# Expert products of two mixture-of-experts layers in full fp32, on column halves of the array, with a ring of 14 expert blocks

## What is computed

```python
def moe(h, router_w, router_b, w_gate, w_up, w_down):
    x = h.reshape(-1, D)                          # 256 x 1024
    aff = jax.nn.sigmoid((x @ router_w).astype(jnp.float32))
    ...                                           # best of 4 groups of experts, then the best 2 experts in it
    w = aff * chosen
    w = (w / w.sum(-1, keepdims=True)).astype(x.dtype)
    y = jnp.zeros_like(x)
    for e in range(N_EXPERTS):                    # 16; gate and up 1024 x 512, down 512 x 1024
        he = (jax.nn.silu(x @ w_gate[e]) * (x @ w_up[e])) @ w_down[e]
        y = y + w[:, e:e + 1] * he
```

## Time and profile before

| | |
|---|---|
| runs | 1465.07, 1466.48 and 1457.2 us, median 1465.07 |
| span of the profiled execution | 1454.6 us (its own time is not given apart from the span; the median is 10.5 us above it) |
| PE, DVE, ACT busy | 1381.8, 1126.3, 932.6 us |
| mean granted TensorE clock | 0.982 |
| DMA | 342.63 MB, mean 236 GB/s |
| chain that ended last | PE 78%, DVE 11%, ACT 5%, DMA 3% |

### The profile page before, as it was taken

The page is one execution under the profiler, slowest core; times in us unless marked ns, Lnnn a source line. Parts: engine busy times, 40 slices in busy tenths (PEclk is TensorE's granted clock), DMA queues, the critical chain, the costliest instruction groups (busy, mean ns, idle before and its releaser), DMA issues.

```text
span 1454.6 us, 18747 instructions
## 1 busy us (share of the span) xinstructions
PE 1381.8 (95%) x7320; PEld 1146.0 (79%) x7320; DVE 1126.3 (77%) x1351; ACT 932.6 (64%) x1103; POOL 72.7 (5%) x78
## 2 busy tenths in 40 slices
PE   7999998999999899999899999979999998799998
PEld 5887886888888677666788888857788887699986
DVE  4765578999999777677999999976665557578872
ACT  4453545989898643584789898955545664356561
POOL 0000000000000000000000000000773000000000
PEclk9999998999999999998999999999999999899999
DMA  9644544999999934503699999956445434455550
GB/s 338 198 146 145 198 164 154 390 376 391 387 398 401 351 127 139 185 1 145 239 396 384 380 394 398 398 213 202 145 146 173 146 117 145 155 178 187 191 172 31
DMA packets 128477, 342.63 MB, mean 236 GB/s; under 512 B 10189, under 2 KB 17021, under 8 KB 111869
## 3 DMA queue, kind: packets, MB, share of 16 engines
q1 hardware_dynamic: 121632, 331.57, 62.8%
q10 hardware_dynamic: 6748, 9.77, 2.0%
HBM read 340.27 MB, written 1.05 MB: 235 GB/s over the span
## 4 chain that ended last, share of the span: by engine, by line
PE 78%; DVE 11%; ACT 5%; DMA 3%; issue 2%; ACTq 1%; DVEq 0%
PE PS L656 22%; PE PS L1287 17%; PE PS L503 9%; PE PS L581 6%; DVE wlo L468 5%; PE PS L559 5%; PE PS L1326 3%; ACT whi L462 3%; PE PS L1276 2%; DMA raw<-in_moe_w_gate 2%; PE PS L1364 2%; PE PS L1360 1%; PE PS L2023 1%; PE PS L1750 1%; PE PS L1776 1%
## 5 line engine op out<-in xcount | busy, mean ns | idle before, releaser
L468 DVE TENSOR_TENSOR wlo<-raw,whi 128x2048 fp32r<-128x2048 f32 x314 | 706.8, 2274 | 122.4 <-ACT whi L462 116.4
L462 ACT ACTIVATE whi<-raw 128x2048 fp32r<-128x2048 f32 x314 | 589.8, 1897 | 44.4 <-PE PS L559 17.3
L1287 PE MATMUL PS<-whi,xg 128*128 128x512 f32 x512 | 205.6, 402 | 0.0
L1287 PE MATMUL PS<-wlo,xg 128*128 128x512 f32 x512 | 200.5, 392 | 0.0
L656 PE MATMUL PS<-whi,th 128*128 128x512 f32 x480 | 193.5, 403 | 2.1 <-DVE wlo L468 2.0
L656 PE MATMUL PS<-whi,tl 128*128 128x512 f32 x480 | 190.2, 396 | 0.0
L656 PE MATMUL PS<-wlo,th 128*128 128x512 f32 x480 | 189.3, 394 | 0.0
L1287 PEld LDWEIGHTS PS<-whi,xg 128*128 128x128 f32 x512 | 96.4, 188 | 18.6
L1287 PEld LDWEIGHTS PS<-wlo,xg 128*128 128x128 f32 x512 | 96.3, 188 | 18.6
L656 PEld LDWEIGHTS PS<-whi,th 128*128 128x128 f32 x480 | 90.2, 188 | 25.1 <-issue 2.4
L656 PEld LDWEIGHTS PS<-whi,tl 128*128 128x128 f32 x480 | 90.1, 188 | 21.8
(11 more groups left out here) (404 smaller groups left out, 2264.9 us busy)
## 6 DMA issues: line engine op xcount, KB each, us to landing
raw<-in_moe_w_gate SPq DMA_DIRECT2D x64, 1024.0 KB, 7.5
raw<-in_moe_w_up SPq DMA_DIRECT2D x64, 1024.0 KB, 8.4
raw<-in_moe_w_down SPq DMA_DIRECT2D x64, 1024.0 KB, 7.7
raw<-in_w_in SPq DMA_DIRECT2D x32, 1024.0 KB, 5.2
raw<-in_ret_w_in SPq DMA_DIRECT2D x24, 1024.0 KB, 5.1
raw<-in_w_up SPq DMA_DIRECT2D x20, 1024.0 KB, 5.1
raw<-in_w_down SPq DMA_DIRECT2D x10, 1024.0 KB, 5.0
raw<-in_ret_w_out SPq DMA_DIRECT2D x8, 1024.0 KB, 5.0
```

Of the source, the lines that this page charges most:

```text
L462: nc.scalar.activation(s.whi[:, high, 0:kc, 0:wide], s.raw[:, slot, 0:kc, 0:wide], ACT.Copy).then_inc(s.hi_done, 1)
L468: nc.vector.tensor_tensor(s.wlo[:, slot, 0:kc, 0:wide], s.raw[:, slot, 0:kc, 0:wide], s.whi[:, high, 0:kc, 0:wide], ALU.subtract).then_inc ...
L1287: last = nc.tensor.matmul(PS[:, bank, :], stationary(c), w[:, q, c, :], start=(start and c == 0 and k == 0), stop=(stop and c == KC - 1 an ...
```

## The change

- `xg` and `hT` are kept in fp32 and not split; gate, up and down are multiplied in fp32, straight from the loaded blocks: `split_hi` and `split_lo` of expert blocks are gone (192 of the 314 pairs of splits).
- The stationary operand has 64 columns. Gate's output goes to partitions 0 to 63 of a PSUM bank and up's to 64 to 127 of the same bank (`gate_and_up`), so the two use different column halves of the array and follow each other chunk by chunk. In `down` the two halves of the output's columns stand in the same way in bank 6.
- ACT takes Silu from the one half, DVE multiplies by the other (both 64x512), 4 transposes turn the result (`turned_hidden`), ACT copies it to `hT`. The fold matmuls are gone.
- `y_split` holds, per half, the high part in 64 partitions and the low part in the other 64, so `scatter` needs 4 matmuls.
- Order on PE for an expert: gate and up, gather, scatter of the last expert, transposes of hidden, slot weights of the next expert, down.
- The blocks of an expert lie in a ring of 14: the 7 slots of `raw`, the 5 of `whi`, and two more. Counts of their own (`moe_ready`, `moe_used`) serve it; the blocks of the linear behind wait for the last use of their place (`after_experts`). Down's blocks are now 256 whole rows, two per partition, one run of 8 KB.
- The output stages ahead of a layer no longer split two expert blocks.

```diff
+MOE_SLOTS = 14
...
-        xg = A("xg", [P, 2, DC, PER, 2, SLOTS], F32R)
+        xg = A("xg", [P, 2, DC, PER, SLOTS])
...
+        moe_more = A("moe_more", [P, MOE_SLOTS - RAWS - HIGHS, KC, BW])
...
+        moe_homes = [("raw", 0), ("raw", 1), ("raw", 2), ("high", 0), ("raw", 3), ("high", 1), ("raw", 4), ("high", 2),
+                     ("raw", 5), ("high", 3), ("raw", 6), ("high", 4), ("more", 0), ("more", 1)]
...
         def out_and_norm_scalar(act, l, layer):
 
-            for i in (2, 3, 4):
+            for i in (2, 3):
                 split_hi(act, sweep_first, l.b0 + i, 0)
             early_table(ACT.Sqrt)
             root_half(act, 4 * layer, 0)
-            split_hi(act, sweep_first, l.b0 + 5, 0)
...
             residual_half(dve, o, l, 0, 0)
-            split_lo(dve, sweep_first, l.b0 + 4, 0)
             residual_half(dve, o, l, 0, 1)
...
             residual_half(dve, o, l, 1, 0)
-            split_lo(dve, sweep_first, l.b0 + 5, 0)
...
+            return [g[0:half], u[0:half], g[half:], u[half:], d[0:SEQ], d[SEQ:]]
 
         def paired_sync(sp, layer):
             b0 = moe_b0[layer]
-            for n, (e, i) in enumerate(paired_order()):
-                load_block(sp, sweep_first, b0 + n, 0, [(expert_blocks(layer, e)[i], KC, 0, BW)], block_rows(i))
+            for n in range(MOE_BLOCKS):
+                kind, k = moe_homes[n % MOE_SLOTS]
+                if n >= MOE_SLOTS:
+                    sp.wait_ge(moe_used, MOE_BLOCKS * layer + n - MOE_SLOTS + 1)
+                elif kind == "raw":
+                    sp.wait_ge(block_used, b0 + k - RAWS + 1)
+                elif kind == "high":
+                    sp.wait_ge(block_used, b0 + k - HIGHS + 1)
+                else:
+                    sp.wait_ge(block_used, b0)
...
+            def gate_and_up(e, half):
+
+                g, u = 6 * e + 2 * half, 6 * e + 2 * half + 1
+                moe_landed(pe, layer, 3 * e + half)
...
+                pe.wait_ge(s.xg_done, xg_count(layer, e // PER, 2 * half + 1))
+                if half == 0 and e >= 2:
+                    pe.wait_ge(s.hT_done, v0 + e - 1)
                 for c in range(KC):
...
+                    x = xg[:, (e // PER) % 2, KC * half + c, e % PER, :]
+                    for k, n in enumerate((g, u)):
+                        m = nc.tensor.matmul(PS[64 * k:64 * k + 64, gate_up_bank(e), :], x, moe_place(layer, n)[:, c, :],
+                                             start=(half == 0 and c == 0), stop=(half == 1 and c == KC - 1),
+                                             skip_group_check=True)
...
+            def down(e):
+                pe.wait_ge(s.hT_done, v0 + e + 1)
+                if e >= 1:
+                    pe.wait_ge(s.y_lo, 2 * (v0 + e))
+                moe_landed(pe, layer, 3 * e + 2)
+                for b in range(2):
+                    n = 6 * e + 4 + b
+                    for c in range(2):
+                        for half in range(2):
+                            m = nc.tensor.matmul(PS[64 * half:64 * half + 64, 6, :], hT[:, 2 * b + c, :],
+                                                 moe_place(layer, n)[:, 2 * c + half, :], start=(b == 0 and c == 0),
+                                                 stop=(b == 1 and c == 1), skip_group_check=True)
+                    m.then_inc(moe_used, 1)
...
                     for half in range(2):
-                        for y in (y_h, y_l):
-                            last = nc.tensor.matmul(PS[:, 2 * tt + half, :], pickT[:, e % 3, tt * P:(tt + 1) * P],
-                                                    y[:, half, :], start=False, stop=False,
-                                                    skip_group_check=True)
+                        last = nc.tensor.matmul(PS[:, 2 * tt + half, :], pickT[:, e % 3, tt * P:(tt + 1) * P],
+                                                y_split[:, half, :], start=False, stop=False, skip_group_check=True)
```

More of the change, by code:

```diff
@@ L357, in block_program @@
         sweep_first = Ring(*ring)
[L358 removed]
+        sweep_second = [Sweep(f"second{i}", ([sem(f"raw_ready{k}_second{i}") for k in range(RING // 2)],
                                              sem(f"hi_done_second{i}"), sem(f"lo_done_second{i}"),
@@ L1254, in fill_of, with moe_place, moe_landed @@
-        def fill_of(e):
-            return (e + 1) // PER + 1, (e + 1) % PER
+        def moe_place(layer, n):
+            kind, k = moe_homes[n % MOE_SLOTS]
+            if kind == "raw":
+                return moe_ring[:, (moe_b0[layer] + k) % RAWS]
+            if kind == "high":
+                return moe_ring[:, RAWS + (moe_b0[layer] + k) % HIGHS]
+            return moe_more[:, k]
+        def moe_landed(eng, layer, pair):
+            lanes = MOE_SLOTS // 2
+            before = sum(1 for m in range(MOE_BLOCKS // 2) if m % lanes == pair % lanes)
+            eng.wait_ge(moe_ready[pair % lanes], 32 * (before * layer + pair // lanes + 1))
@@ L1280, in gather @@
                 last.then_inc(s.gathered, 1)
-            def product(bank, e, i, stationary, start, stop):
-                b = b0 + place[e, i]
-                pe.wait_ge(ring.lo_done, b + 1)
-                for c in range(KC):
-                    for k, (w, q) in enumerate(((whi, b % HIGHS), (wlo, b % RAWS))):
-                        last = nc.tensor.matmul(PS[:, bank, :], stationary(c), w[:, q, c, :],
-                                                start=(start and c == 0 and k == 0),
-                                                stop=(stop and c == KC - 1 and k == 1))
-                last.then_inc(ring.block_used, 1)
@@ L1307, in slot_weights, with turned_hidden @@
+            def turned_hidden(e):
+                pe.wait_ge(s.h_done, v0 + e + 1)
+                rows = hidden[0:SLOTS, :].rearrange("p (b q c) -> p b c q", b=2, c=2)
+                for k in range(4):
+                    m = nc.tensor.transpose(PS[:, gate_up_bank(e), k * SLOTS:(k + 1) * SLOTS], rows[:, k // 2, k % 2, :],
+                                            cst[0:SLOTS, C_ID:C_ID + SLOTS])
+                m.then_inc(s.h_turned, 1)
             def slot_weights(e, bank):
-                if e >= 1:
-                    pe.wait_ge(s.gate_out, v0 + e)
@@ L1346, in paired_tensor @@
                     pe.wait_ge(s.pickT_ready, v0 + 1)
[L1347 to L1377 removed]
+                down(e)
             scatter(E - 1)
@@ L1450, in paired_scalar @@
-                if e + 1 < E:
-                    gate_out(e + 1)
-                split(n[4])
+                    act.wait_ge(s.h_turned, v0 + e)
+                nc.scalar.activation(hidden[SLOTS:2 * SLOTS, :], PS[0:SLOTS, gate_up_bank(e), :],
+                                     ACT.Silu).then_inc(s.silu_done, 1)
+                if e == 0:
+                    turned_pick(0, 6)
+                act.wait_ge(s.h_turned, v0 + e + 1)
+                if e >= 1:
+                    act.wait_ge(moe_used, MOE_BLOCKS * layer + 6 * e)
@@ new lines, in paired_vector, with y @@
+        def paired_vector(dve, s, layer):
+            v0 = E * layer
+            def y(e):
+                for half in range(2):
+                    rows, low = slice(64 * half, 64 * half + 64), slice(64 - 64 * half, 128 - 64 * half)
+                    dve.wait_ge(s.y_hi, 2 * (v0 + e) + half + 1)
+                    nc.vector.scalar_tensor_tensor(y_split[low, half, :], PS[rows, 6, :], w_slot[rows, e:e + 1],
+                                                   y_split[rows, half, :], ALU.mult, ALU.subtract).then_inc(s.y_lo, 1)
```

302 lines of the change are left out of this document (115 added, 187 removed).

## The result

The changed kernel takes 1377.56 us (median of 4 runs, 1374.49 to 1378.99) against 1463.46 us for the kernel before (4 runs, 1457.2 to 1466.48) on the same chip: ratio 0.9419, 95% interval 0.9394 to 0.9445. The forecast was 1381 us, the range 1362 to 1420.

What follows compares the result with a forecast made beforehand. The prediction took DMA, DVE and PE, all full in the expert stages, to bound the kernel. With 42.6 us less per layer, counted as twice 42 or 84 us, 1465 - 84 gave 1381 us, range 1362 to 1420.

Steps and rivals of the forecast that it cites:

- Three full resources: Expert stages before: DMA, DVE and PE are full at once, one expert taking 16.0 us; a change must relieve all three.
- four blocks at 423 and two at 352 are 15.9 us: Expert transfers before: four blocks at 423 GB/s (2.48 us each) and two at 352 (2.98) alone explain the period.
- A pair at 0.86: Expert products on PE: two 64-high fp32 matmuls on the two column halves together take 0.86 us, bounds 0.855 and 1.71.
- Rival (c): Expert products: column halves do not run together at 512 columns; expert 23.8 us, 122 us more per layer, 1709 us; 6%.
- Rival (d): Expert products: weight loads stand open, 6.5 us more per expert, 63 us more per layer, 1591 us; 3%.
- One expert 13.6 us: PE after the change: one expert sums to 13.6 us, 13.3 for the last four, 16 experts 216.5; bounds 13.0 and 14.6.
- Start 240.1, scatter 458.9: Layer 0 after the change: gate and up begin at 240.1 us, scatter at 458.9 against 501.51, 42.6 us less.
- PE ends last: Layer's end: PE finishes at 456.6 us; DMA's block 95 lands at 448.6, wanted at 454.5; PE last by 6 us.
- rival (a): Expert transfers: DMA ends last, blocks keep 2.67 us; 33 us less per layer, 1399 us; 20%.
- 84 us of span: Both expert layers: twice 42 us saved, 84 us in all.
- stage that shrinks while the linear behind it grows: Sign that the forecast is wrong: the expert stage gets shorter while the linears behind it get longer; no size given.
- those 10.5: Whole kernel: the 10.5 us between the profiled span, 1454.6, and the median of three runs, 1465.07, were forecast to stay.

Runs made afterwards that it cites:

- e8: Kernel before, with VectorE's expert-stage subtraction cut to 8 columns and the high part multiplied a second time in place of the low: 1455.84 us.
- e11: Kernel before, with only down's transfers turned into 8 KB runs: 1459.31 us.
- e5: Changed kernel, with up's products written to the same 64 output rows as gate's, so both use one column half: 1591.47 us.
- e3: Changed kernel, with a ring of 8 expert blocks in place of 14: 1405.68 us.
- e10: Changed kernel, with half of the gate and up products left out and transfers as they are: 1370.01 us.
- e2: Changed kernel, with down's blocks loaded as column halves again, in 2 KB runs: 1387.63 us.
- e1: Changed kernel, with all four of gate's products of a half ahead of up's four: 1432.38 us.
- e6: Changed kernel, with gate's products for two chunks, then up's for the same two, so halves alternate by two matmuls: 1377.59 us.
- e7: Kernel before, with VectorE's expert-stage subtraction cut to 8 columns and the products with the low part left out: 1442.79 us.
- e12: Kernel before, with the subtraction cut to 8 columns, the low-part products left out and down's blocks in 8 KB runs: 1438.81 us.

## Why the prediction was right, point by point

**Three full resources: right in its use, wrong in its count.** VectorE, TensorE and the transfers had little or no room, and relieving VectorE or the transfers alone gives nothing or little (e8, e11). The step "four blocks at 423 and two at 352 are 15.9 us: the transfers alone explain the period" fails: without VectorE and TensorE in the way the same transfers ran at 402 GB/s (15.65 us), and short runs cost 408 against 421. And "a change must relieve all three" left out the fourth, ScalarE, at 90 us of 100. The forecast did not suffer, since the change empties ScalarE too, and the sum was made for the kernel after, not as a difference of bounds.

**A pair at 0.86: right, 0.87 measured.** Rival (c), 6%, would have needed one thing to be otherwise, and e5 shows that thing's price for gate and up: a stage of 330 us against 220. Rival (d) fell with the pitch; the loads of L1340 take 137 ns each and stand beside the products. The rule of the Trainium skill (TensorE: Matmul & The Clock Gate, Part 3, "What overlaps and what doesn't") that a load overlaps only where the row group differs is not what these runs show: both halves of L1340 use all 128 rows, and the period holds no open load.

**One expert 13.6 us: 13.72.** Gather 1.06 for 0.95, scatter 1.05 for 0.93, transposes 0.62 for 0.43, against 0.3 set aside for changes of mode. PE's wait for hidden is 0.00 with a gather and 0.32 without, for hT 0.47 in the last expert alone. The 16 experts took 239.78 to 456.5, 216.7 us; forecast 216.5.

**Start 240.1, scatter 458.9: 239.78 and 459.17.**

**Transfers: the rate right, the margin wrong.** 423 GB/s was forecast, 421 came. "PE ends last" holds, but "by 6 us" fails by 4: the last block landed at 451.15, not 448.6, at 2.50 us a block for 2.48, and it was wanted at down's start, 453.07, not at 454.5. The same slip stands in rival (a), with "half of down 1.7 and the tail 2.3" behind the last block: down runs whole behind it, and e3 shows 6.1 us from down's start to the scatter. That the forecast time held all the same is in part luck, since a last block 2 us later would have set the end. A cheaper pair would have gained little: e10 takes away 112 us of products and gains 7.5. Rival (a), the transfers last at 2.67 us a block, did not come: down's old rate was neither its runs alone nor a law; e2, with 408 GB/s (2.57 us a block), is where it would have led, 1388 us. The 358 GB/s that the Trainium skill gives (DMA: Bandwidth & Descriptors, "Where 436 GB/s comes from") does not fit the 421 that the window of 100 us shows on this one core.

**84 us of span, 79.9 measured.** By layer 0's last scatter 42.3 us were gained, by that of layer 1 83.4 (958.87 to 875.50); 3.5 were given back behind layer 1, where VectorE starts late. That is the "stage that shrinks while the linear behind it grows" in small. DVE's removed splits at the output, taken at 0 to 4.5 us a layer, are not seen as a gain.

**1381 us: closer than its parts.** The forecast kept "those 10.5" us between the span and the median. They were no cost of the program: 1.8 us lie between a run's time and its span, and the rest is that the profiled execution of before was among the shortest. After, the median is 2.9 above the span. So the span was forecast 4.1 us too short and what stands on it 7.6 too long, and the two leave 3.4 us of error. That part is luck.

## What to carry to other kernels

When a stage's period is explained by one resource, read every engine's number in the window, also the one at 90%: with several at 90 to 100%, relieving one or three of them gives 0 to 20 us of the 86 that all together give. Two products whose outputs are 64 high can be had for the price of one by giving each its own column half, and the order in which they are written matters little so long as the partner is within a few instructions. Where a stage's transfers are slower than its products, as here (14.9 to 13.7 us), each block of a deeper ring is worth its transfer time once per stage, less the margin that the products leave: 6 blocks in two stages gave 28 us. Where a product waits for two blocks together, the last one is wanted at its start.

## What the runs showed of the hardware that I had not expected

- TensorE starts work for the free column half ahead of the queue's order, by about four records (e1), and runs of four records need no turn-taking (e6).
- A DMA share of 1.00 is no proof that transfers are at their limit: 384 GB/s at 1.00, 402 at 1.02 (e7), 406 at 1.00 (e12), 421 at 1.01 (after), with 8 KB and 2 KB runs in each kind of kernel. In the kernel before it rose when the engines were relieved (384 to 402) and not when the runs were made longer (383, e11).
- VectorE's first instruction behind layer 1 starts 1.67 to 1.69 us after an 8 KB packet of an instruction queue has landed, in six runs whose transfers are busy there, and up to 4.96 us after its last one.
- Part of what a lighter PE wins goes to the clock: in e10 the granted clock fell to 0.51 behind waits of 3.04 and 0.99 us, and down took 5.33 us instead of 3.65.
